# Input panels of a recurrence with features on partitions in place of transposes, and an earlier token-scale row

## The reference, cut to what matters

```python
def second_block(x, norm_gain, w_in, ...):
    xn = rmsnorm(h, norm_gain[l])
    proj = jnp.einsum('bsd,de->bse', xn, w_in[l])
    q, k, v, g_sb, x_lru, g_lru = jnp.split(proj, ...)      # 1024 columns each
    ...
    xc = causal_depthwise_conv(x_lru, conv_w[l], conv_b[l]) # 4 taps over the tokens
    y_lru = rg_lru(xc, lru_w_a[l], ...)
    y_lru = y_lru * jax.nn.silu(g_lru)
```

## Time and profile before

| | us |
|---|---|
| median of 3 runs | 1406.52 |
| lowest and highest | 1406.46, 1407.52 |
| the profiled execution, its device time | 1406.4 |
| the span of its trace | 1404.3 |

### The profile page before, as it was taken

How to read it: one execution, slowest core, us unless ns; L and a number is a source line. 1 busy time by engine, 2 the same in 40 slices (tenths; PEclk the granted TensorE clock), 3 DMA queues, 4 the chain that set the end, 5 groups by cost and what they waited for, 6 DMA issues and landing times.

```text
span 1404.3 us, 18031 instructions
## 1 busy us (share of the span) xinstructions
PE 1396.9 (99%) x7332; PEld 1245.7 (89%) x7332; DVE 880.7 (63%) x935; ACT 736.8 (52%) x881; POOL 34.2 (2%) x58
## 2 busy tenths in 40 slices
PE   9999999999999999999999999999999999999999
PEld 7898888888899889998899888998888888898988
DVE  6775565665565655665566655565667687567854
ACT  7745555454554444454444534454564657667542
POOL 2000000000000000000000000000000001000000
PEclk9999999999999999999999999999999999999999
DMA  9555555566556565655666666665655565545573
GB/s 363 194 192 177 181 193 183 195 234 216 194 196 205 200 206 200 203 201 202 202 205 200 200 205 201 204 199 192 206 186 189 173 218 169 191 168 166 187 235 132
DMA packets 78706, 279.53 MB, mean 199 GB/s; under 512 B 9184, under 2 KB 10208, under 8 KB 78240
## 3 DMA queue, kind: packets, MB, share of 16 engines
q1 hardware_dynamic: 76176, 273.12, 58.4%
q0 software_dynamic: 864, 3.41, 0.7%
q10 hardware_dynamic: 1584, 1.85, 0.4%
HBM read 276.24 MB, written 2.10 MB: 198 GB/s over the span
## 4 chain that ended last, share of the span: by engine, by line
PE 98%; DVE 1%; DMA 0%; ACT 0%; issue 0%; SPq 0%; ACTq 0%; DVEq 0%
PE banks L546 24%; PE banks L510 20%; PE banks L511 20%; PE banks L513 20%; PE banks L563 5%; PE banks L596 3%; PE banks L644 1%; PE banks L741 1%; DMA raw<-in_weights 0%; PE banks L632 0%; PE banks L754 0%; PE banks L671 0%; PE banks L770 0%; PE banks L781 0%; PE banks L531 0%
## 5 line engine op out<-in xcount | busy, mean ns | idle before, releaser
L1249 DVE TENSOR_TENSOR w_lo<-raw,w_hi 128x1024 fp32r<-128x1024 f32 x508 | 619.6, 1224 | 475.8 <-ACT w_hi L885 471.1
L885 ACT ACTIVATE w_hi<-raw 128x1024 fp32r<-128x1024 f32 x508 | 535.4, 1056 | 614.3 <-PE banks L513 386.0
L510 PE MATMUL banks<-w_hi,xb 128*128 128x512 f32 x764 | 290.2, 380 | 0.0
L511 PE MATMUL banks<-w_lo,xb 128*128 128x512 f32 x764 | 289.6, 379 | 0.0
L513 PE MATMUL banks<-w_hi,xb 128*128 128x512 f32 x764 | 289.6, 379 | 0.0
L546 PE MATMUL banks<-xa,w_hi 128*128 128x512 f32 x1024 | 242.3, 379 | 0.0
L510 PE MATMUL banks<-w_hi,xa 128*128 128x512 f32 x560 | 213.5, 381 | 0.0
L511 PE MATMUL banks<-w_lo,xa 128*128 128x512 f32 x560 | 212.2, 379 | 0.0
L513 PE MATMUL banks<-w_hi,xa 128*128 128x512 f32 x560 | 212.2, 379 | 0.0
L546 PEld LDWEIGHTS banks<-xa,w_hi 128*128 128x128 f32 x1024 | 184.3, 190 | 20.8
L513 PEld LDWEIGHTS banks<-w_hi,xb 128*128 128x128 f32 x764 | 144.4, 189 | 20.5
(11 more groups left out here) (237 smaller groups left out, 846.6 us busy)
## 6 DMA issues: line engine op xcount, KB each, us to landing
raw<-in_weights SPq DMA_DIRECT2D x510, 512.0 KB, 3.9
h<-in_x SPq DMA_DIRECT2D x2, 1024.0 KB, 9.2
arena<-in_x_turned SPq DMA_DIRECT2D x6, 256.0 KB, 7.1
result<-stage ACTq DMA_DIRECT2D x6, 256.0 KB, 4.3
raw<-in_weights SPq DMA_DIRECT2D x4, 256.0 KB, 3.9
arena<-in_final_norm POOLq DMA_DIRECT2D x1, 1024.0 KB, 6.5
arena<-in_w_gate_up POOLq DMA_DIRECT2D x1, 512.0 KB, 7.2
arena<-in_gla_b_gate POOLq DMA_DIRECT2D x1, 512.0 KB, 8.2
```

What stands on the lines that cost most here:

```text
L510: pe.matmul(o, xh[:, kt, xs], woven(w_hi, slot, k), start=kt == 0, stop=False)
L511: pe.matmul(o, xh[:, kt, xs], woven(w_lo, slot, k), start=False, stop=False)
L885: act.activation(w_hi[:, n % RING, :, :], raw[:, n % RING, :, :], ACT.Copy)\
L1249: dve.tensor_tensor(w_lo[:, n % RING, :, :], raw[:, n % RING, :, :], w_hi[:, n % RING, :, :].bitcast(F32), ALU.subtract).then_inc(lo_ready, 1)
```

## The change

Panels 48 and 49 take the feature form: `multiply_x`, after the pattern of `multiply_query`, with the banks of `X_BANKS`. Their transposes, the copies to `stage` and the moves from the transposed banks go away. In their place ScalarE copies the second half of the banks to `stage` (`cross_x`), and VectorE adds the first half to it and writes `lru_x` (`add_x`): pair 0 in chunk 7 of the panel itself, pair 1 after its end. TensorE waits for `x_added` before it writes pair 0 of panel 49, and before panel 50.

The token scale is not in `lru_x` then. It is put in afterwards, in chunk 3 of the next panel, by one VectorE instruction that multiplies all of `lru_x` by `gate_row` (and by 2, as the row holds half the scale). So the row is made earlier: the copies to `row_from` in panel 49, chunk 0, `turn_scale` after its chunk 1, in bank 4 (`tp`) and not bank 6, and the copy to `gate_row` in chunk 2. `gate_row` gets a buffer of its own outside the arena, and is kept for the gate panels. The weights of panels 48 and 49 are laid out in HBM without weaving (`panels` in place of `woven`), in the same number of bytes.

```diff
+X_BANKS = {48: (0, 6), 49: (0, 2)}
...
+        gate_row = sb("gate_row", [P, S])
...
-        gate_row = room(15360, S)
...
 # TensorE
+                if KINDS[t] == "x":
+                    multiply_x(t, c).then_inc(chunk_used, 1)
+                    return
+                if t == FIRST_X + 2 and c == 0:
+                    pe.wait_ge(x_added, 3)
...
             def turn_scale():

                 pe.wait_ge(row_ready, 1)
-                pe.wait_ge(lru_th, 8)
+                pe.wait_ge(tp_hi, groups_before(FIRST_X + 1))
+                pe.wait_ge(tp_lo, groups_before(FIRST_X + 1))
                 for tt in range(TT):
-                    last = pe.matmul(aux[:, 0, tt * P:(tt + 1) * P], row_from[:, tt, :], ident[:, :],
+                    last = pe.matmul(tp[:, 0, tt * P:(tt + 1) * P], row_from[:, tt, :], ident[:, :],
...
+            def multiply_x(t, c):
+
+                slot = (CH * t + c) % RING
+                for pair in (1, 0) if c == 0 else (0, 1):
+                    if t == FIRST_X + 1 and c == 0 and pair == 0:
+                        pe.wait_ge(x_added, 1)
+                    for w, width in ((w_hi, 2 * S), (w_lo, S)):
+                        for k in range(CK):
+                            kt = CK * c + k
+                            for i in range(2):
+                                j = 2 * pair + i
+                                last = pe.matmul(
+                                    banks[:, X_BANKS[t][pair] + i, 0:width], w[:, slot, k, j * P:(j + 1) * P],
+                                    xa[:, kt, 0:width // S, :].rearrange("p h (a b) -> p h b a", a=TT),
+                                    start=w is w_hi and kt == 0, stop=w is w_lo and kt == KT - 1)
+                    if c == CH - 1 and pair == 0:
+                        last.then_inc(x_half, 1)
+                return last
...
-                if t == 54 and c == 7:
+                if t == FIRST_X + 1 and c == 1:
                     turn_scale()
-                if t >= 1 and prev in "roDxKQ" and c == late:
+                if t >= 1 and prev in "roDKQ" and c == late:
                     turn_panel(t)
...
 # ScalarE
+            def cross_x(q, pair):
+
+                bank, own = X_BANKS[q][pair], slice(2 * pair, 2 * pair + 2)
+                act.activation(by_tile(stage_z(q % 2)[:, own, :]), unwoven(banks[:, bank:bank + 2, S:2 * S]),
+                               ACT.Copy).then_inc(x_cross, 1)
...
-                    if prev in "xKQ":
-                        if q == FIRST_X:
-                            act.wait_ge(r2_ready, 1)
+                    if prev == "x":
+                        panel_done(act, t)
+                        cross_x(q, 1)
+                        act.wait_ge(x_cross, 2 * (q - FIRST_X) + 2)
+                        act.sem_inc(acc_read_act, 1)
+                        act.sem_inc(stage_act, 1)
+                    if prev in "KQ":
...
-                        if prev == "x" and g == 0:
-                            if q == FIRST_X + 1:
-                                act.wait_ge(conv_ready, 1)
-                            move_first(lru_x[:, 0:2, PAD:PAD + S], G)
...
-                if t == 55 and c == 0:
+                if KINDS[t:t + 1] == "x" and c == CH - 1:
+                    act.wait_ge(x_half, t - FIRST_X + 1)
+                    cross_x(t, 0)
+                if t == FIRST_X + 1 and c == 2:
                     act.wait_ge(row_turned, 1)
-                    act.wait_ge(ms_ready, ST_ALL)
-                    act.activation(gate_row, aux[:, 0, 0:S], ACT.Copy).then_inc(row_out, 1)
+                    act.activation(gate_row[:, :], tp[:, 0, 0:S], ACT.Copy).then_inc(row_out, 1)
...
 # VectorE
+            def add_x(q, pair):
+
+                bank, own = X_BANKS[q][pair], slice(2 * pair, 2 * pair + 2)
+                dve.wait_ge(x_cross, 2 * (q - FIRST_X) + pair + 1)
+                if q > FIRST_X:
+                    dve.wait_ge(conv_ready, 1)
+                dve.tensor_tensor(lru_x[:, own, PAD:PAD + S].rearrange("p j (a b) -> p j a b", a=TT),
+                                  unwoven(banks[:, bank:bank + 2, 0:S]),
+                                  by_tile(stage_z(q % 2)[:, own, :]), ALU.add).then_inc(x_added, 1)
...
-                    if prev in "xKQ":
+                    if prev == "x":
+                        add_x(q, 1)
+                        dve.wait_ge(x_added, 2 * (q - FIRST_X) + 2)
+                        dve.sem_inc(acc_read_dve, 1)
+                        dve.sem_inc(stage_dve, 1)
                         if q == FIRST_X:
                             dve.wait_ge(r2_ready, 1)
+                            dve.memset(lru_x[:, :, 0:PAD], 0.0)
+                            for tt in range(TT):
+                                ins = dve.tensor_copy(row_from[:, tt, :],
+                                                      scl[:, R2H + tt:R2H + tt + 1].to_broadcast([P, P]))
+                            ins.then_inc(row_ready, 1)
+                    if prev in "KQ":
...
-                        if prev == "x" and g == 1:
-                            if q == FIRST_X:
-                                link(dve.memset(lru_x[:, :, 0:PAD], 0.0))
-                            move_second(lru_x[:, 2:4, PAD:PAD + S], G)
-                if t == 54 and c == 6:
-                    for tt in range(TT):
-                        ins = dve.tensor_copy(row_from[:, tt, :], scl[:, R2H + tt:R2H + tt + 1].to_broadcast([P, P]))
-                    ins.then_inc(row_ready, 1)
+                if prev == "x" and c == 3:
+                    dve.wait_ge(row_out, 1)
+                    link(dve.scalar_tensor_tensor(
+                        out=lru_x[:, :, PAD:PAD + S], in0=gate_row[:, :].unsqueeze(1).to_broadcast([P, 4, S]), scalar=2.0,
+                        in1=lru_x[:, :, PAD:PAD + S], op0=ALU.mult, op1=ALU.mult))
+                    dve.sem_inc(tp_hi, 2)
+                    dve.sem_inc(tp_lo, 2)
...
+                    if KINDS[t:t + 1] == "x" and c == CH - 1:
+                        add_x(t, 0)
                     if t < PANELS:
                         split_lo(t, c)
```

More of the change, by code:

```diff
@@ L69, in turned @@
     done -= 2 * sum(done > groups_before(t) for t in (3, 4))
-    return done - CH if done <= groups_before(FIRST_U + 1) - 4 else done - CH - 2 * KINDS.count("u")
+    if done > groups_before(FIRST_U + 1) - 4:
+        done -= 2 * KINDS.count("u") + 2 * sum(done + 4 > groups_before(t) for t in (FIRST_X + 1, FIRST_X + 2))
+    return done - CH
 QUERY_BANKS = {2: (0, 4), 3: (0, 2)}
+X_BANKS = {48: (0, 6), 49: (0, 2)}
 GATE_BANKS = {56: (0, 4), 57: (2, 0), 58: (4, 2), 59: (0, 4)}
@@ L261, in gated_block_kernel @@
         r1_ready = sem("r1_ready")
+        x_half, x_cross, x_added = sem("x_half"), sem("x_cross"), sem("x_added")
         q_half, q_cross, q_added = sem("q_half"), sem("q_cross"), sem("q_added")
@@ L1031, in before @@
                         act.activation(xb_hi[:, k:k + 2, :], stage_u(b, g), ACT.Copy).then_inc(tp_hi, 1)
-                if prev and prev in "roDx" and c == (4 if prev == "D" or prev == "r" and t < FIRST_O else 3):
+                if prev and prev in "roD" and c == (4 if prev == "D" or prev == "r" and t < FIRST_O else 3):
                     for g in range(2):
@@ L1405, in before @@
                             .then_inc(stage_dve, 1)
-                    if prev in "xKQ":
+                    if prev == "x":
[3 more added lines that the diff above has]
+                        dve.sem_inc(stage_dve, 1)
                         if q == FIRST_X:
                             dve.wait_ge(r2_ready, 1)
-                        half_panel(t, stage[:, b, 1, :], scl[:, R2 + 1:R2 + 2])
[L1410 to L1414, removed]
+                            dve.memset(lru_x[:, :, 0:PAD], 0.0)
[4 more added lines that the diff above has]
+                    if prev in "KQ":
+                        half_panel(t, stage[:, b, 1, :], scl[:, R2 + 1:R2 + 2])
+                        dve.wait_ge(stage_act, count("qxKQ", q))
+                        dve.sem_inc(kq_sq, 1)
                     if prev == "V":
@@ L1424, in before @@
                             dve.wait_ge(row_out, 1)
-                        dve.tensor_tensor(gate_z, gate_z, gate_row.unsqueeze(1).to_broadcast([P, 4, S]), ALU.mult)\
+                        dve.tensor_tensor(gate_z, gate_z, gate_row[:, :].unsqueeze(1).to_broadcast([P, 4, S]), ALU.mult)\
                             .then_inc(gate_scaled, 1)
@@ L1646, in before @@
                     taps = CONV_TAPS[j].get(CH * (t - FIRST_X - 1 - j) + c, ())
[L1647 to L1651, removed]
+                    if 3 in taps and j == 1:
+                        dve.wait_ge(lru_mm, 4)
                     for w in taps:
@@ L1823, in lay_out @@
         parts.append(woven(a["mlp_w_down"][0][b * D:(b + 1) * D], 0, 4))
-    parts += [woven(in_2, first, 2) for first in (4096, 1024, 0, 2048)]
+    parts.append(panels(in_2, 4096, 2))
```

(1 more changed line is left out.)

## The result

The changed kernel takes 1409.55 us (median of 20 runs, 1407.54 to 1410.24), the kernel before 1406.74 (20 runs, 1405.76 to 1407.52): +2.8 us, a ratio of 1.0016 with a 95% interval of 1.0011 to 1.0022. The twenty times lie in two clusters. Six are from 1407.54 to 1408.44, with a mean granted clock of TensorE of 1.000. Fourteen are from 1409.30 to 1410.24, with 0.999 or 0.998. The profiled execution took 1410.24 and is one of the fourteen. The forecast of 1407.9 describes the six and misses the fourteen.

What follows compares the result with a forecast made beforehand. TensorE was taken to bound the kernel (busy 99%, 98% of the chain). Terms -1.74 + 0.47 + 0 + 2.69 = +1.42 on the profiled 1406.4 gave 1407.9 us, range 1405.2 to 1409.6.

Steps and rivals of the forecast that it cites:

- The four terms: Transposes removed -1.74, new panel form +0.47, turn_scale moved 0, TensorE's waits on x_added +2.69; sum +1.42 us.
- Transposes: Panels 49 and 50: two sets of eight leave TensorE's path, 0.87 us each, -1.74 in all.
- The new form: Input panels as half-chunks, 16 matmuls a chunk for 12: 0.03 us a chunk, 16 chunks, +0.47.
- turn_scale: Moves from panel 54 to after chunk 1 of panel 49; costs 0.45 us in either kernel, its wait met: 0.
- The wait: Start of panel 50: TensorE stands 2.59 us for VectorE's late add, plus 0.10 at restart: +2.69.
- The covers: Waits met in time: 0.3 us spare at panel 48's end, scaling hidden by 0.15, conv_lo 1.4 early, weight loads 0.
- Rival (b): The pause at panel 50 takes TensorE's clock down; 3 us of work at low level gives +4.4, 1410.9; chance 0.07.
- the prediction's own signs: Forecast wrong if the gap at panel 50 is missing, over 3.1 us, or the first matmuls after it step by 0.43.
- PEclk 9 throughout: Expected in the profile after: TensorE's granted clock at 9 in every slice of the page.
- (c): Larger VectorE backlog: the first x_added wait fails too and scaling is not hidden; +2.5 us, 1409.0; chance 0.13.
- Rival (a): The add for panel 50 is not late, or hardly: 1405.2 with no wait, 1405.9 with VectorE free; chance 0.10.

Runs made afterwards that it cites:

- the other banks: Changed kernel with pair 0 of both input panels in PSUM banks 6 and 7, no wait at panel 50: 1405.43 us, again 1405.15.

## Why the prediction was right and where it was wrong

**The four terms held.** Transposes: 0.87 a set was worked out, and 0.88 measured where they were put back. The new form: panel 48 takes 0.23 more, and the forecast was 0.47 for two such panels; the row of the query panels decides. By the spacing in the Trainium skill, TensorE: Matmul & The Clock Gate, section Back-to-back issue gap, which the section gives for the isolated gap between matmuls, it would have been 0.08 a panel, and the trace does not agree. turn_scale: 5.24 after the start of panel 49 (1068.05 less 1062.81), 0.36 and a longer next step, no wait. The wait: with 0 at panel 49's start at 1062.81, the splits for chunks 5 and 6 were expected at 20.98, and start at 20.98; the add was expected at 23.26, and starts at 23.25; TensorE was expected at 24.00, and starts at 24.08. The stall is 2.68, where 2.59 was worked out, plus 0.07 in the next step.

**The covers held.** At the first boundary the add ended at 1063.63, 0.82 after panel 49's start, and pair 0 began at 1064.12: no gap, 0.5 to spare. The scaling of the first panel ran at 1073.61 and was over before the split at 1075.09, which waited 0.26 for ScalarE; from the earlier trace rows it had been 0.15 to spare. conv_lo ended at 1094.96 and the gate matmuls that wait for it began at 1096.42, 1.46 later; in the second trace with the other banks, where TensorE doesn't stall, the two are 0.90 apart (1090.48 and 1091.38). The weight loads held nobody up. The six runs at full clock, 1407.54 to 1408.44 around the forecast 1407.9, and the removal of the wait, -1.4 and -1.6 for the worked-out -1.27, confirm the sum for executions in which the clock stays.

**The step that failed is the choice among the cases.** Rival (b), that the pause takes the clock down, was given 0.07, and it came true in 14 of 20 runs, and so it set the median. By the prediction's own signs the forecast is wrong in the profiled execution: the matmuls behind the gap step by 0.43. (Its other sign, PEclk 9 throughout, held and shows nothing, for the reason given above.) The ground for the low chance was the earlier trace rows: a gap of 1.60 at full clock. It was one execution, and near the edge: 1.37 left the clock alone in 11 of 11 runs, 1.90 took it down in 6 of 11. The pause of 2.6 that the prediction had just worked out was longer than any in the trace, so no row spoke against the fall, and 0.07 had no ground. The size of (b) was off as well: 3 us of work at half clock were assumed, and 1.68 of loss is what the profile shows, so the fourteen have their middle at 1409.8 and not at 1410.9, and the median of all twenty is 1409.55. It lies inside the range by 0.05 only, and that is luck. The range's upper end had been set by (c), a larger backlog, which did not occur, and (b) had been left out of it. The measured +2.8 is twice the forecast +1.4, and right at the 0.2% that parted same from slower.

Rival (a) fell with the gap of 2.51. That the wait with its fall of the clock is what costs, and not the panels' form or the layout, was argued before and is shown by the other banks, with the one open point of the start.

## What to carry to other kernels

Where a buffer is handed over, ask what stands ahead of the releasing instruction in its engine's order, not how long it takes itself: a backlog of 3.5 us on VectorE was harmless until TensorE waited for something behind it. The same removal of transposes came to -1.5 us or +2.8, depending on a table of banks and the wait that goes with it. In these runs a pause of TensorE of 1.9 us and more had a second price, 1.7 us in each trace that has it, paid in a part of the runs. If a pause can't be removed, work in it that nobody needs paid for itself here: +1.1 and +1.4, not +2.7.

## What the runs showed of the hardware

The granted clock fell in a part of the executions only, by the mean to three decimals: never with a gap of 1.37 (0 of 11), in about half with 1.9 to 2.0 (10 of 22), in 21 of 31 with 2.5, in 6 of 11 with 3.2, in 8 of 9 with 3.65. It can fall more than 1 us after matmuls have resumed (restart 1086.30, slow from about 1087.5); with the gap of 3.65 the first matmul behind it was slow already (1087.33 to 1087.77). The price of a fall is nearly the same in the four traces that have one: 1.68 (gap 2.51), 1.69 (3.65), 1.69 (1.90) and 1.68 (3.15), all counted from the restart to the first matmul at full pace. Single runs lost more: 1412.96 with the gap of 3.65 and 1412.94 with 3.16, at mean clocks of 0.998 and 0.997, and no trace shows how. The changed kernel has two clusters of times 2.0 us apart (1407.8 and 1409.8 in the middle of each), 0.3 more than the traces' price, and a single run of it says little. Transposes of the identity (1 of 11 down) and plain matmuls (0 of 11) in the gap kept the clock up alike, as far as 11 runs each can tell.
